# A gated recurrent stage in which the next unit's projections move behind the first levels and the states' products, and two engines take their work in another order

## What is computed

```python
def hg_forget(z, lb):
    k = (1.0 - lb) * jax.nn.sigmoid(-z)
    logf = jnp.log(jnp.maximum(lb + (1.0 - lb) * jax.nn.sigmoid(z), TINY))
    return k, logf
...
    def step(s, inp):
        qc, kc, vc, gc = inp
        b = jnp.cumsum(gc, axis=2)
        inter = jnp.einsum('bhtk,bhkv->bhtv', qc * jnp.exp(b), s)
        diff = b[:, :, :, None, :] - b[:, :, None, :, :]
        decay = jnp.where(causal, jnp.exp(jnp.minimum(diff, 0.0)), 0.0)
        scores = jnp.einsum('bhtk,bhtsk,bhsk->bhts', qc, decay, kc)
        intra = jnp.einsum('bhts,bhsv->bhtv', scores, vc)
...
    q = jax.nn.silu(split_heads(p[..., O_Q:O_G].astype(F32))) * HG_DK ** -0.5
    o = hgrn2_bidir(q, v, k_f, k_b, lf_f, lf_b, s0_f, s0_b)
    o = o * lax.rsqrt(jnp.mean(o * o, axis=-1, keepdims=True) + EPS) * hg_norm_g
    hg = (o.reshape(o.shape[0], o.shape[1], HG_WIDTH) * jax.nn.silu(p[..., O_G:O_SC].astype(F32))).astype(p.dtype)
```

## Time and profile before

| | us |
|---|---|
| median of 3 runs | 2868.96 |
| lowest, highest | 2861.96, 2872.52 |
| the profiled execution's own time | 2870.58 |
| its span | 2868.8 |
| the stage's start and units, within the span | about 1430 to 1991 |

### The profile page before, as it was taken

The page is one execution under the profiler, slowest core; times in us unless marked ns, Lnnn a source line. Parts: engine busy times, 40 slices in busy tenths (PEclk is TensorE's granted clock), DMA queues, the critical chain, the costliest instruction groups (busy, mean ns, idle before and its releaser), DMA issues. The chain is left out here.

```text
span 2868.8 us, 39160 instructions
## 1 busy us (share of the span) xinstructions
PE 2536.4 (88%) x16521; PEld 1372.7 (48%) x16713; DVE 1631.0 (57%) x2112; ACT 959.8 (33%) x1109; POOL 34.5 (1%) x61
## 2 busy tenths in 40 slices
PE   7978685999999999998857979795987999999997
PEld 4446462444444444443545756665433444444443
DVE  6667745654444443445336676767566767666253
ACT  5115205432232231323244555454243222222121
POOL 0020000010000000000000000000000000000000
PEclk9989797999999999999879999997998999999998
DMA  9036363211211124332000000000211112122433
GB/s 309 23 102 195 104 208 118 59 40 49 58 44 55 47 65 111 87 88 76 23 26 15 23 23 23 16 8 15 59 30 30 44 44 58 44 58 81 116 101 99
DMA packets 299447, 198.99 MB, mean 69 GB/s; under 512 B 11280, under 2 KB 294062, under 8 KB 298799
## 3 DMA queue, kind: packets, MB, share of 16 engines
q1 hardware_dynamic: 298438, 196.70, 23.1%
q10 hardware_dynamic: 873, 0.32, 0.0%
HBM read 187.02 MB, written 9.45 MB: 68 GB/s over the span
## 5 line engine op out<-in xcount | busy, mean ns | idle before, releaser
L198 PE MATMUL ps<-hT,arena 128*128 128x512 bf16 (+1 forms) x6241 | 1379.6, 380 | 78.5 <-DVE hT L697 18.0
L198 PEld LDWEIGHTS ps<-hT,arena 128*128 128x128 bf16 x6384 | 627.4, 99 | 822.9 <-issue 51.8
L1883 PE MATMUL ps<-arena 128*128 128x512 bf16 x2069 | 455.5, 379 | 4.2 <-DVE arena L1865 1.9
L1883 PEld LDWEIGHTS ps<-arena 128*128 128x128 bf16 x2112 | 206.3, 98 | 251.4 <-DVE arena L1865 3.8
L2137 DVE SCALAR_TENSOR_TENSOR arena<-ps,vec,arena 128x945 f32<-128x945 f32 (+2 forms) x176 | 215.1, 1222 | 75.5 <-ACT arena L2123 56.2
L2104 DVE SCALAR_TENSOR_TENSOR arena<-ps,vec,arena 128x1023 f32<-128x1023 f32 (+1 forms) x88 | 106.7, 1275 | 181.4 <-ACT arena L2094 181.4
L1865 DVE TENSOR_TENSOR arena<-hT,arena 128x2816 bf16<-128x2816 f32 (+2 forms) x44 | 93.7, 2156 | 156.9 <-ACT arena L1859 156.7
L2766 PE MATMUL ps<-arena 128*128 128x128 f32 x896 | 126.0, 301 | 55.3 <-DVE arena L3036 46.2
L1859 ACT ACTIVATE arena<-hT 128x2816 bf16<-128x2816 f32 (+2 forms) x44 | 77.8, 1798 | 251.0 <-DMA hT<-w_down_dram 123.9
L2766 PEld LDWEIGHTS ps<-arena 128*128 128x128 f32 x896 | 119.7, 214 | 62.1 <-DVE arena L3036 49.1
L2050 DVE TENSOR_TENSOR arena<-hT,arena 128x2048 bf16<-128x2048 f32 x44 | 100.9, 2292 | 35.3 <-ACT arena L2016 35.3
(11 more groups left out here) (418 smaller groups left out, 2570.1 us busy)
## 6 DMA issues: line engine op xcount, KB each, us to landing
xT<-ada_w_dram SPq DMA_DIRECT2D x24, 1024.0 KB, 6.0
hT<-w_up_dram SPq DMA_DIRECT2D x44, 512.0 KB, 4.9
hT<-ffn_up_dram SPq DMA_DIRECT2D x44, 512.0 KB, 4.9
hT<-w_down_dram SPq DMA_DIRECT2D x30, 704.0 KB, 6.5
hT<-ffn_down_dram SPq DMA_DIRECT2D x30, 704.0 KB, 7.0
arena<-w_in_dram SPq DMA_DIRECT2D x35, 512.0 KB, 4.0
xT<-w_mod_dram SPq DMA_DIRECT2D x16, 1024.0 KB, 5.3
arena<-w_mod_dram SPq DMA_DIRECT2D x8, 1024.0 KB, 19.6
```

What stands on the lines that cost most here:

```text
L198: last = pe.matmul(out, lhs(a, kt), rhs(b, kt, i), start=start and kt == 0 and (a, b) == (0, 0), stop=stop and kt == n_k - 1 and (a, b) == ...
L1883: last = pe.matmul(self.bank(u), self.part(u, a, kt), self.g[:, b, kt, cols], start=kt == 0 and (a, b) == (0, 0), stop=kt == FT - 1 and (a ...
```

## The change

Nothing is computed otherwise; the same instructions come in another order. On TensorE level 1 now follows level 0, and `ss` and `kv` follow it; Z0 is no longer cut into two halves around the diagonal product and level 0, but stands whole behind `kv`. V0, GATE and QUERY are no longer cut in halves either: V0 stands ahead of level 4, and GATE, V1 and QUERY behind it. The list of slots follows. On ScalarE the levels' Exp come before the fronts of the next unit, the high halves of the weights get a place of their own (`weights_hi`), and `decays` is cut in two. On VectorE the loop over levels is written out in another order. The start of the stage is reordered on ScalarE and VectorE in the same way.

```diff
@@ -2676,10 +2676,10 @@
-        jobs += [(n, "kt", 0), (n, "kt", 1)] + front_of_next(Z0) + [(n, "level", NL), (n, "level", 0)] + \
-                ([(n, "ss", 0)] if d == 0 and h else []) + [(n, "kv", 0), (n, "kv", 1)] + front_of_next(Z1) + \
-                [(n, "level", 1)] + front_of_next(V0, GATE) + [(n, "level", 2), (n, "level", 3)] + front_of_next(V1) + \
-                front_of_next(QUERY) + [(n, "level", l) for l in range(4, NL)]
+        jobs += [(n, "kt", 0), (n, "kt", 1), (n, "level", NL), (n, "level", 0), (n, "level", 1)] + \
+                ([(n, "ss", 0)] if d == 0 and h else []) + [(n, "kv", 0), (n, "kv", 1)] + front_of_next(Z0, Z1) + \
+                [(n, "level", 2), (n, "level", 3)] + front_of_next(V0) + [(n, "level", 4)] + \
+                front_of_next(GATE, V1, QUERY) + [(n, "level", l) for l in range(5, NL)]
...
@@ -2782,14 +2779,13 @@
                 pe.wait_ge(kh_ready, n + 1)
                 for i in range(2):
                     chunk_job((n, "kt", i), halves[i], lambda out, c: pe.transpose(out, kh[:, c, :], k.ident[:, :]))
-                front(n + 1, Z0, (0,))
                 pe.wait_ge(k_ready, n + 1)
                 pe.wait_ge(q_scaled, h + 1)
                 chunk_job((n, "level", NL), range(T // P), lambda out, c: pe.matmul(
                     out, keys[:, n % 2, CTX + c * P:CTX + (c + 1) * P], q[:, h % 2, c * P:(c + 1) * P],
                     start=True, stop=True))
                 level(n, 0)
-                front(n + 1, Z0, (1,))
+                level(n, 1)
                 if d == 0 and h:
                     sum_of_squares(n, h)
                 pe.wait_ge(kt_done, 2 * n + 2)
@@ -2797,13 +2793,9 @@
                 for i in range(2):
                     chunk_job((n, "kv", i), halves[i], lambda out, c: pe.matmul(
                         out, kh_t[:, c, :], vals[:, h % 2, c, :], start=True, stop=True))
+                front(n + 1, Z0)
                 front(n + 1, Z1)
-                level(n, 1)
-                front(n + 1, V0, (0,))
-                front(n + 1, GATE, (0,))
                 level(n, 2)
-                front(n + 1, V0, (1,))
-                front(n + 1, GATE, (1,))
                 level(n, 3)
                 pe.wait_ge(states_ready, n + 1)
                 pe.wait_ge(qh_ready, n + 1)
@@ -2813,10 +2805,10 @@
                     last = pe.matmul(o_ps[:, c * P:(c + 1) * P], states[:, c, :], qh[:, c * P:(c + 1) * P],
                                      start=d == 0 and c % 4 == 0, stop=False, skip_group_check=True)
                 last.then_inc(inter_made, 1)
-                front(n + 1, V1)
-                front(n + 1, QUERY, (0,))
+                front(n + 1, V0)
                 level(n, 4)
-                front(n + 1, QUERY, (1,))
+                for piece in (GATE, V1, QUERY):
+                    front(n + 1, piece)
                 for l in range(5, NL):
                     level(n, l)
                 pe.wait_ge(selected, n + 1)
...
-                if piece in LAST and tile + 2 < 5 * HG_HEADS:
-                    stream.hi(act, tile + 2)
+
+            def weights_hi(n, piece):
+
+                if has(n, piece) and tile_of(n, piece) + 2 < 5 * HG_HEADS:
+                    stream.hi(act, tile_of(n, piece) + 2)
@@ -2889,10 +2884,15 @@
 
                 if n > last_unit:
                     return
-                d = units[n][1]
                 act.wait_ge(kh_sub, n + 1)
                 act.activation(z, z, ACT.Exp).then_inc(kh_exp, 1)
                 level(n, 0)
+
+            def query_decays(n):
+
+                if n > last_unit:
+                    return
+                d = units[n][1]
...
@@ -2917,11 +2917,18 @@
 
             stream.hi(act, 0)
             stream.hi(act, 1)
-            for piece in PIECES[0]:
-                front(0, piece)
+            front(0, Z0)
+            front(0, Z1)
             softplus_parts(0)
+            weights_hi(0, Z1)
+            front(0, V0)
+            front(0, V1)
+            weights_hi(0, V1)
             forget_parts(0)
+            front(0, QUERY)
+            weights_hi(0, QUERY)
             decays(0)
+            query_decays(0)
             for n, (h, d) in enumerate(units):
                 take_out((n, "kt", 0), kh_t[:, 0:8, :].rearrange("p a b -> p (a b)"))
                 signal((n, "kt", 0), kt_done)
@@ -2930,21 +2937,26 @@
                 if d == 0 and h:
                     squares(h - 1)
                 level(n, 2)
-                front(n + 1, Z0)
+                level(n, 3)
                 if d == 0 and h:
                     inverse_root(n)
-                level(n, 3)
+                level(n, 4)
+                front(n + 1, Z0)
                 front(n + 1, Z1)
                 softplus_parts(n + 1)
-                level(n, 4)
+                weights_hi(n + 1, Z1)
+                level(n, 5)
+                level(n, 6)
                 front(n + 1, V0)
+                forget_parts(n + 1)
                 front(n + 1, GATE)
-                forget_parts(n + 1)
-                level(n, 5)
+                weights_hi(n + 1, GATE)
                 front(n + 1, V1)
-                level(n, 6)
+                weights_hi(n + 1, V1)
+                decays(n + 1)
                 front(n + 1, QUERY)
-                decays(n + 1)
+                weights_hi(n + 1, QUERY)
+                query_decays(n + 1)
             squares(HG_HEADS - 1)
...
@@ -3095,48 +3107,56 @@
 
             stream.lo(dve, 0)
             stream.lo(dve, 1)
-            for piece in (Z1, V1, QUERY):
-                weights_lo(0, piece)
-            scale_q(0)
+            weights_lo(0, Z1)
             softplus(0)
+            weights_lo(0, V1)
             forget(0)
             key_distance(0)
             subtract(0, 0)
+            weights_lo(0, QUERY)
+            scale_q(0)
             subtract(0, 1)
             decayed_keys(0)
+            dve.wait_ge(q_scaled, 1)
             for n, (h, d) in enumerate(units):
                 weigh(n, 0)
                 subtract(n, 2)
                 diagonal(n)
-                for l in range(1, NL):
-                    weigh(n, l)
-                    if l + 2 < NL:
-                        subtract(n, l + 2)
-                    select(n, l - 1)
-                    if l == 1:
-                        decayed_queries(n)
-                        chain_states(n)
-                        if d == 0 and h:
-                            finish(h - 1)
-                        weights_lo(n + 1, Z1)
-                    if l == 2:
-                        softplus(n + 1)
-                    if l == 3:
-                        weights_lo(n + 1, GATE)
-                    if l == 4:
-                        forget(n + 1)
-                    if l == 5:
-                        weights_lo(n + 1, V1)
-                        key_distance(n + 1)
-                        subtract(n + 1, 0)
+                weigh(n, 1)
+                select(n, 0)
+                subtract(n, 3)
+                weigh(n, 2)
+                select(n, 1)
+                subtract(n, 4)
+                chain_states(n)
+                decayed_queries(n)
+                weigh(n, 3)
+                if d == 0 and h:
+                    finish(h - 1)
+                weigh(n, 4)
+                select(n, 2)
+                subtract(n, 5)
+                select(n, 3)
+                subtract(n, 6)
+                softplus(n + 1)
+                weights_lo(n + 1, Z1)
+                weigh(n, 5)
+                weigh(n, 6)
+                select(n, 4)
+                forget(n + 1)
+                key_distance(n + 1)
+                subtract(n + 1, 0)
+                weights_lo(n + 1, GATE)
+                weights_lo(n + 1, V1)
+                select(n, 5)
                 subtract(n + 1, 1)
+                decayed_keys(n + 1)
                 scale_q(n + 1)
                 weights_lo(n + 1, QUERY)
                 select(n, NL - 1)
                 s_, use = slot((n, "level", NL - 1))
                 dve.wait_ge(read[s_], use + 1)
                 dve.sem_inc(selected, 1)
-                decayed_keys(n + 1)
             finish(HG_HEADS - 1)
```

More of the change, by code:

```diff
@@ L2732, in _, with front @@
         def _(pe):
-            def front(n, piece, steps=(0, 1)):
+            def front(n, piece):
                 if not has(n, piece):
@@ L2737, in front @@
                 job, tile = (n, "front", piece), tile_of(n, piece)
-                if 0 in steps:
-                    stream.ready(pe, tile)
-                    wait_free(pe, job)
+                stream.ready(pe, tile)
+                wait_free(pe, job)
                 if piece in (V0, V1):
@@ L2743, in front @@
                     for i, c in enumerate(chunks):
[L2744 to L2747, removed]
+                        last = split_matmuls(pe, [banks(job)[:, i * P:(i + 1) * P]],
+                                             lambda s, kt: k.hT[:, s, kt, c * P:(c + 1) * P],
```

(8 more changed lines are left out.)

## The result

| | before | after |
|---|---|---|
| median, us | 2870.74 (4 runs) | 2820.33 (4 runs) |
| lowest, highest | 2861.96, 2872.8 | 2816.74, 2822.98 |
| profiled execution, its span | 2870.58, 2868.8 | 2822.98, 2821.3 |

The ratio is 0.9824, with an interval of 0.9806 to 0.9843. The forecast was 2825.

What follows compares the result with a forecast made beforehand. TensorE, busy 2536.4 of 2868.8 us, was taken as the bound, with gains only in its waits and low-clock work. Start -18.3 and units -27.8 gave -46.1: 2824.5 from 2870.6, forecast 2825, range 2810 to 2848.

Steps and rivals of the forecast that it cites:

- The start: Stage start: softplus of unit 0 begins behind Z1, so the first transposes start at 1475.5 instead of 1493.79, -18.3 us.
- Forward units: From one output product to the next, a forward unit takes 59.3 us against 68.3, as GATE no longer precedes the forget gate.
- 5.8 us for it and the transposes: Start of a forward unit: output product and transposes follow a gap and run at the low clock, 5.8 us together.
- the tail from Z1 to the output product: End of a forward unit: softplus, forget gate, decayed keys and selects on ScalarE and VectorE, from 29.2 to 59.3 us.
- Backward units: A backward unit takes 67.3 us against 64.9, +2.4, with a low-clock start and V0 and QUERY ahead of needed work.
- just hidden: Backward unit's last high half: with a median load landing of 3.9 it ends at 64.4; at 9.2 it would cost 4.8.
- The last unit: It has no fronts and keeps its order but for the states: 32.0 us against 31.8.
- the middle: Low clock of 3.6 us behind each gap, 2825; bounds are no low clock, 2806, and low through the diagonal product, 2838.
- the 5.5 us of unit 0: Unit 0, without a head to finish: 5.5 us to the end of its first diagonal product, within its 55.4.
- one sign of being wrong: Wrong if units exceed 68 us, forward VectorE waits long at level 4 or 5, or low clock outlasts the diagonal product.
- Rivals 3 to 5: 3: high clock after gaps, 2806 (0.05); 4: low through `kv`, 2875 (0.05); 5: through half of Z0, 2911 (0.02).
- Rivals 1 and 2: 1: only the start pays, backward units lose the forward gain, 2852 (0.10); 2: the start pays little, 2843 (0.08).

Runs made afterwards that it cites:

- gate_first: Changed kernel with ScalarE taking GATE and its high half of weights ahead of the forget gate's functions again: 2862.7 us, ratio 0.9975.
- weigh_late: Changed kernel with VectorE's `weigh` of levels 5 and 6 and `select` 4 behind the forget gate again: 2838.4 us, ratio 0.9892.
- backward: Changed kernel, backward units: forget gate's functions ahead of V0's take, forget gate ahead of `select` 4, levels 5 and 6 and last `select` moved earlier: 2800.2 us.
- filler: Changed kernel with 34 (forward) or 20 (backward) extra unused matmuls in the gap ahead of each output product: 2800.2 us, ratio 0.9755.
- the three versions after it: On those moves: extra matmuls in forward gaps, 2790.6 us; instead forward levels, selects and decayed keys earlier, 2789.6; the latter plus 20 extra matmuls, 2790.2.

## Why the prediction was right

**The start.** Forecast -18.3, measured -18.1. The steps came out nearly one for one: counted from QUERY's start, the decayed keys end at 20.7 in the trace, where I had 1475.4 - 1454.9 = 20.5.

**Forward units.** Forecast 59.3; measured 57.4, 58.7 and 55.9. Two terms were mis-sized. The first is "5.8 us for it and the transposes": in units 2 and 6 it was 4.5, since the clock rose at the output product's end, and 5.7 in unit 4. The granted clock in three stretches of the changed kernel:

```profile
1601.90:1605.30 3.40, 3.40 (x16) 0.52 0.50 147
1605.30:1606.40 1.10, 1.10 (x13) 1.00 0.00 0
...
1729.10:1731.20 2.10, 2.10 (x11) 0.50 0.00 0
```

At 1729.1 the same transposes still ran at 0.50, and that unit took 58.7. The second is the tail from Z1 to the output product, forecast 30.1, measured 29.4 in units 2 and 4 and 28.0 in the last forward unit. That one has no further weight tiles to split, which I hadn't counted. The mechanism was the one named: gate_first and weigh_late put the two waits back.

**Backward units.** Forecast 67.3; measured 66.9, 66.2 and 66.9. That they'd be slower than before (64.9) is right, and so are both causes: backward took V0 and QUERY out of the chain and got 4.3 to 6.4 us a unit; filler removed the low clock and got 1.8 to 2.5. The late load behind the last low half did no more than I wrote ("just hidden"): in unit 1 ScalarE waits 1.6 us for it, and VectorE doesn't wait.

**The last unit.** Forecast 32.0, measured 33.8; the prediction doesn't show the working of the 32.0. In the trace, level 3 waits 4.79 us for `weigh` 3, which now stands behind `chain_states`, and takes 3.78 at a granted clock of 0.50, instead of 1.95 at the high one; that alone is 1.8.

**The sum.** Units: -27.8 forecast, -34.1 measured. Of the 6.3 between them the forward units are 5.8 and the backward ones 1.9, and the last unit is 1.8 the other way. The profiled execution came to 2823.0 against 2824.5, but that closeness is luck: 4.2 us of scatter ahead of the stage hid most of the 6.3. Between medians the gain is 50.4 us, where 2825 against 2869.0 had meant 44.

**The low clock.** Of the bounds, the middle was right: low for all seven output products behind a gap and for the transposes of four of them (2.07 to 2.34 us; 1.25 to 1.40 in the other three); in one (1729.1 to 1731.2) to the diagonal product's start. Behind the start's gap of 10.5 us it was low through the diagonal product (3.62), which the 5.5 us of unit 0 had counted. By its letter, one sign of being wrong did appear: the clock was low beyond the diagonal product at level 3 of the last unit, once. Short waits of 0.7 us ahead of level 1 in every unit didn't hold the clock down, so the rule that I cited from the Trainium skill (TensorE: Matmul & The Clock Gate, A second HAM failure mode: psum-queue depth-cycling) doesn't show in this trace. In `backward` and the three versions after it, though, a wait of 2.05 us ahead of level 0 stretched levels 0 and 1 from 3.81 to 5.44 us in 3 of 12 cases, so short waits aren't always free. Rivals 3 to 5 fall by the changed kernel's trace; filler shows that rival 3's price of 19 us was about right (16.1 in the units, 20.1 in the medians), although the event didn't occur.

**Rivals 1 and 2.** Both fall: the units gave 34.1 us and the start 18.1. In rival 1 one step was wrong. For 27.8 us to be lost in three backward units, each must lose 9.3 us more, nearly four times the 2.4 and not three.

## What to carry to other kernels

Where three in-order queues feed one another, ask for each wait what is queued behind it: here ScalarE waited for a long projection that nobody needed soon, with the head of the next chain behind it, and that one order was worth 42 us. Put work that only fills time behind the chain's work on every queue, and let the next unit's chain start where it needs only what is ready. Then look at what the moved work now holds up: with QUERY last on TensorE its take on ScalarE delayed that of the transposes, 2 us each time. Laying the queues side by side with durations from the trace gave the size within a few us, including the part that gets slower.

## What I had not expected

A gap of 5.1 us could cost as much low-clock time as one of 8.4 (3.78 and 2.34 us at 1725.50, 3.79 and 1.40 at 1659.30), and the price differed by 1.3 us between units of one execution with the same gap (transposes 1.26 us at 1605.30 and 2.34 at 1729.08, both behind a gap of 5.1). And filling a gap with matmuls that nothing needs was worth 20 us in one order, 9.5 in another and nothing in a third: it pays only where TensorE's first products behind the gap are on the path.
